# One stage for merge and output product, a search that turns bits by exclusive or, and units placed anew

## The chip, the cores and the metric

One core of a Trainium2 chip runs the whole program. The metric is the device time of one execution in microseconds (us). Three timed runs of the kernel before lie between 3658.96 and 3662.44, with a median of 3660.72. The engines are named as in the profile: PE is TensorE, DVE is VectorE, ACT is ScalarE, POOL is GpSimd and SP is SyncE, which only issues DMAs here. "Clock" is the TensorE clock that was granted, as a share of full speed.

## The reference

Two transformer blocks run one after the other on 2048 tokens of width 1024. The first block selects 256 keys for each query by an index score before it attends; the second has a sliding window. Both end in the same two products: a gated merge of two branches, and an output product.

```python
def first_block(x, ...):
    proj = rms_norm(x) @ w_in
    iscore = sum_h relu(qi_h @ ki.T) * wi_h          # 8 index heads, causal by chunks of 64
    idx = top_k(iscore, 256)                         # attention over these keys alone
    a = dsa_attention(...) * silu(z_a)
    b = multiscale_pool(u_b, ...) * silu(z_b)
    g = sigmoid(gates + merge_bias)
    y = g[0] * (a @ w_branch_a) + g[1] * (b @ w_branch_b)
    return x + y @ w_out

def second_block(x, ...):
    ...
    merged = gate_a * (y_a @ w_proj_a) + gate_b * (y_b @ w_proj_b)
    y = merged @ w_out
    return x + gate * rms(y, g_post)
```

All values are float32. The kernel gets close to float32 by splitting each operand into a high part (rounded to the fp32r type) and a low part (the rest), and by three matmuls: high by high, high by low, low by high.

## The kernel before, in words

The program is a chain of phases, each with its own buffers and its own block of instruction streams, joined by semaphores. Two kinds of phase are touched.

**phase_first** computes the z, u and gate columns of the input projection (the "units"), the index scores, and the key masks. There are 112 units: 56 for each half of the tokens. A unit is 128 columns by 512 tokens, that is 8 steps of k with three matmuls each, 24 matmuls of 128x512. A "place" is one block of 128 weight columns; it serves two units. Its weights are loaded (w_raw), rounded by ACT (w_hi, line 1043) and the low part (w_lo) is a subtraction, made by DVE (line 1115) where it falls in an index stretch and by POOL (line 1033, four instructions of 128x256) elsewhere. There are three slots for split weights, so place m can be split when place m - 3 is done. The low part is needed two places, or about four units, after its slot came free.

The 16 query tiles are handled in two halves of seven (two short tiles need no search). Each half has an index stretch and a try stretch:

- Index stretch: 88 "heads". PE multiplies queries by up to 1024 keys (line 1260) into one of two PSUM buffers, ACT applies relu (line 1066) into one of two buffers, DVE scales and adds (line 1133 for the first head, 1136 for the others). Units are laced between the heads on PE by `slices`; their PSUM is emptied by ACT (lines 1053, 1055, 1057), and a z unit has one more DVE multiplication (line 1124). `IDX_UNITS` says which units stand in the stretch, `FROM` from which head on.
- Try stretch: a search for the 256th largest score of every query, bit by bit, 32 tries. In each try ACT counts three tiles by Sign with an accumulated sum (line 1073), DVE counts four tiles by a comparison (line 1145), and then three short DVE instructions of 128x7 make the next level: `enough` (line 1161), `prefix` (1165) and `level` (1168). The next try's counts wait for it. `TRY_UNITS` says which units stand beside the tries; PE streams them without a wait on the search, but ACT empties their PSUM (four buffers) only between its counts, in the order of `beside_try`.

After the tries, `settle` (lines 1175 to 1184) corrects the level, and `make_mask` (lines 1194 to 1205) makes one mask per tile: for half 0 in front of the heads of half 1, for half 1 at the end of the phase. The order on each engine is the order in which the program emits it; nothing is planned at run time. The activations of a half (p_hT) are loaded again for half 1: SP issues these loads when it comes to units 53 and 56.

**phase_output** runs once for each block, as two blocks of streams with separate buffers. `merge_branches` takes 32 units (4 groups of 512 tokens by 8 column blocks), 24 matmuls each, with the weights as the stationary operand; DVE multiplies by the gates (line 1814) and adds (1816) into yT. `output_product` then loads w_out in eight pieces of 512 KB through two slots (line 1685), rounds them on ACT (1690), makes the low parts in turn on DVE (1696) and POOL (1702), splits y by tile (1904, 1886) and multiplies: 16 tiles of 128 tokens, 48 matmuls each (lines 1948 to 1950) with y as the stationary operand, into one of two PSUM buffers. The first pass over k goes as far as the weights are there.

Of the kernel before, what the change touches and what calls it, by code (L numbers as in the profile page):

```python
# [12 lines left out]
ALU = mybir.AluOpType  # L13
# [803 lines left out]
def phase_first(c, stack):  # L817
# [38 lines left out]
    IDX_UNITS = [(0, 21), (57, 77)]  # L856
    TRY_UNITS = [(21, 57), (77, 107)]
# [42 lines left out]
    cand = sb("cand", [P, NB], I32)  # L900
# [4 lines left out]
    enough = sb("enough", [P, NB], I32)  # L905
# [27 lines left out]
    with nc.Block() as block:  # L933
# [90 lines left out]
        def _(pool):  # L1024
# [87 lines left out]
        def _(dve):  # L1112
# [35 lines left out]
            def begin(half, step):  # L1148
# [3 lines left out]
                nc.vector.memset(prefix[:], 0)  # L1152
# [3 lines left out]
            def attempt(half, j, step):  # L1156
                for b in range(NACT, NB):
                    last = count(half, b, ALU.is_lt)
                step(last)
                dve.wait_ge(counted, half * TRIES + j + 1)  # L1160
                step(nc.vector.tensor_tensor(enough[:], counts[:], wanted[:], ALU.is_le))
                if j == 0:
                    step(nc.vector.tensor_scalar(turned_bits[:], enough[:], -1.0, None, ALU.add))
                else:
                    step(nc.vector.scalar_tensor_tensor(out=prefix[:], in0=enough[:], scalar=TRY_OF[j - 1], in1=prefix[:],
                                                        op0=ALU.logical_shift_left, op1=ALU.bitwise_or))
                if j < TRIES - 1:
# [3 lines left out]
                    dve.wait_ge(cand_ready, half * TRIES + j + 2)  # L1171

            def settle(half, step):
# [3 lines left out]
                step(nc.vector.tensor_tensor(cand[:], prefix[:], upd[:], ALU.add))  # L1177
                step(nc.vector.tensor_tensor(level[:].bitcast(I32), cand[:], turned_bits[:], ALU.bitwise_xor))
# [533 lines left out]
def phase_output(c, stack, second):  # L1712
# [3 lines left out]
    sb, _, _ = c.alloc(stack, "o2" if second else "o1")  # L1716
    yT = sb("yT", [P, KD, SEQ], F32)
    with ExitStack() as inner:
        merge_branches(c, inner, second, yT)
    with ExitStack() as inner:  # L1720
        output_product(c, inner, second, yT)


# [753 lines left out]
```

## Time and profile before

| | us |
|---|---|
| median of three timed runs | 3660.72 |
| the profiled execution | 3663.65 |
| its span, first to last instruction | 3661.9 |
| PE busy | 3227.8 (88%) |
| DVE busy | 1772.6 (48%) |
| ACT busy | 1566.7 (43%) |
| POOL busy | 1162.2 (32%) |
| mean granted clock | 0.927 |

Busy time is a mean over stages with different limits. A share of 88% on PE says that PE is the engine to look at first; it does not say that it is the limit in each stage. The phases that the change touches are phase_first, from about 336 to 1127 us, and the two output phases, from about 1697 to 2130 and from about 3215 to the end.

### The profile page before, as it was taken

To read this page: it belongs to the slowest core of one execution; us is meant where nothing else is said; L and a number is where in the kernel's file an instruction comes from. 1 tells how busy PE (TensorE), PEld (TensorE's weight loads), DVE (VectorE), ACT (ScalarE), POOL (GpSimd) and SP (SyncE) were. 2 spreads that over 40 slices of the span, in tenths; PEclk is the share of its full clock that TensorE was granted. 3 is DMA by queue.
4 is the path that set the end of the run, shared out by engine and by line. 5 is a ranking of instruction groups with operands and counts; after the bars stand their busy time and mean duration, and the time that the engine had idled before them with its cause. 6 is when DMAs were issued, how large, how long until landed. Compare 5 with 4: busy or idle time off the path is not lost. (4 is left out here: it accounts for less than half of the span.)

```text
span 3661.9 us, 43478 instructions
## 1 busy us (share of the span) xinstructions
PE 3227.8 (88%) x15878; PEld 2639.9 (72%) x15878; DVE 1772.6 (48%) x3727; ACT 1566.7 (43%) x2453; POOL 1162.2 (32%) x780
## 2 busy tenths in 40 slices
PE   3996999789983999967897959997999999978799
PEld 3995888677773677755675848886888888856587
DVE  3775679988995666532331126661312132123222
ACT  2444568756973677721101023333444354420111
POOL 2441002200222899922212223332222222232132
PEclk9997999999996999967998969998999999989899
DMA  4566333433324111055543244546444634354422
GB/s 113 173 194 210 119 98 92 146 119 90 92 81 135 61 61 37 27 175 192 144 104 115 92 138 141 159 135 222 124 128 153 208 122 134 110 146 124 117 84 92
DMA packets 419821, 458.19 MB, mean 125 GB/s; under 512 B 30896, under 2 KB 301744, under 8 KB 417968
## 3 DMA queue, kind: packets, MB, share of 16 engines
q1 hardware_dynamic: 419632, 455.72, 40.4%
q8 instruction: 113, 1.85, 0.2%
q14 instruction: 76, 0.62, 0.1%
HBM read 289.70 MB, written 165.94 MB: 124 GB/s over the span
## 5 line engine op out<-in xcount | busy, mean ns | idle before, releaser
L1411 POOL TENSOR_SCALAR a_prob<-a_prob,a_inv 128x128 f32<-128x128 f32 (+15 forms) x128 | 384.2, 3020 | 96.3 <-DVE a_inv L1452 96.2
L1243 PE MATMUL p_pr<-p_hT,p_w_hi 128*128 128x512 f32 x896 | 359.2, 401 | 27.3 <-POOL p_w_lo L1033 26.9
L2324 PE MATMUL p_pr<-p_hT,p_w_hi 128*128 128x512 f32 x896 | 352.2, 393 | 17.6 <-DMA p_hT<-s_hT 17.6
L1244 PE MATMUL p_pr<-p_hT,p_w_hi 128*128 128x512 f32 x896 | 356.3, 398 | 0.0
L1245 PE MATMUL p_pr<-p_hT,p_w_lo 128*128 128x512 f32 x896 | 355.5, 397 | 0.0
L2325 PE MATMUL p_pr<-p_hT,p_w_hi 128*128 128x512 f32 x896 | 350.3, 391 | 0.0
L2326 PE MATMUL p_pr<-p_hT,p_w_lo 128*128 128x512 f32 x896 | 349.7, 390 | 0.0
L758 PE MATMUL t_pj_ps<-t_w_hi,t_hT_slot 128*128 128x356 f32 (+2 forms) x768 | 274.1, 357 | 41.0 <-POOL t_w_lo L474 26.6
L1033 POOL TENSOR_TENSOR p_w_lo<-p_w_raw,p_w_hi 128x256 fp32r<-128x256 f32 x132 | 93.1, 736 | 651.9 <-ACT p_w_hi L1043 651.9
L1073 ACT ACTIVATE p_relu<-p_isc,p_level 128x2048 int8<-128x2048 f32 (+5 forms) x192 | 276.7, 1442 | 43.2 <-DVE p_level L1168 41.8
L1833 PE MATMUL m_b_ps<-m_in_hi,m_w_hi 128*128 128x512 f32 x512 | 214.1, 418 | 77.2 <-POOL m_in_lo L1791 46.2
L760 PE MATMUL t_pj_ps<-t_w_hi,t_hT_slot 128*128 128x356 f32 (+2 forms) x768 | 266.8, 347 | 0.0
L759 PE MATMUL t_pj_ps<-t_w_lo,t_hT_slot 128*128 128x356 f32 (+2 forms) x768 | 266.6, 347 | 0.0
L1432 DVE CUSTOM_DVE_ANT_0 a_prob<-a_s_ps,a_mask 128x512 f32<-128x512 f32 (+3 forms) x320 | 188.5, 607 | 152.3 <-PE a_s_ps L1511 148.8
L1948 PE MATMUL f_o_ps<-f_w_hi,f_y_hi 128*128 128x512 f32 x512 | 207.1, 404 | 42.3 <-POOL f_w_lo L1702 22.0
L2171 POOL TENSOR_TENSOR p_w_lo<-p_w_raw,p_w_hi 128x1024 fp32r<-128x1024 f32 x56 | 136.3, 2434 | 330.4 <-ACT p_w_hi L2193 330.4
L1511 PE MATMUL a_s_ps<-a_kT,a_qT 128*128 128x512 f32 (+3 forms) x640 | 197.8, 414 | 35.9 <-DMA a_kT<-s_kT 30.8
L1145 DVE TENSOR_SCALAR_CACHE_REDUCE p_ranks<-p_isc,p_level 128x1792 uint8<-128x1792 f32 (+4 forms) x130 | 223.0, 1752 | 2.6 <-DVE p_level L1153 0.4
L1243 PEld LDWEIGHTS p_pr<-p_hT,p_w_hi 128*128 128x128 f32 x896 | 172.6, 193 | 69.1 <-POOL p_w_lo L1033 31.3
L1490 ACT ACTIVATE a_pt<-a_t_ps 128x512 f32<-128x512 f32 x272 | 153.7, 593 | 134.2 <-PE a_t_ps L1523 133.6
L2324 PEld LDWEIGHTS p_pr<-p_hT,p_w_hi 128*128 128x128 f32 x896 | 168.8, 188 | 58.2 <-POOL p_w_lo L2171 14.8
L1834 PE MATMUL m_b_ps<-m_in_lo,m_w_hi 128*128 128x512 f32 x512 | 209.1, 408 | 0.0
(270 smaller groups left out, 7142.2 us busy)
## 6 DMA issues: line engine op xcount, KB each, us to landing
p_w_raw<-in_w_in SPq DMA_DIRECT2D x112, 512.0 KB, 4.3
s_hT<-t_hT_slot SPq DMA_DIRECT2D x32, 1024.0 KB, 5.9
p_hT<-s_hT SPq DMA_DIRECT2D x64, 512.0 KB, 9.8
s_gT<-p_o_sb SPq DMA_DIRECT2D x128, 256.0 KB, 4.9
m_gates<-s_gT SPq DMA_DIRECT2D x64, 512.0 KB, 4.9
s_qT<-t_qT_slot SPq DMA_DIRECT2D x32, 512.0 KB, 2.7
s_zuT<-p_o_sb SPq DMA_DIRECT2D x64, 256.0 KB, 5.0
pl_wada<-in_w_ada SPq DMA_DIRECT2D x6, 2048.0 KB, 14.1
```

Source lines behind the costliest of these rows:

```text
L758: nc.tensor.matmul(o, hi, wh, start=(k == 0), stop=False)
L759: nc.tensor.matmul(o, hi, wl, start=False, stop=False)
L760: last = nc.tensor.matmul(o, lo, wh, start=False, stop=(k == KD - 1))
L1073: last = nc.scalar.activation(unread[:, o:o + w], isc[:, o:o + w], ACT.Sign, scale=-1.0, bias=level[:, b:b + 1], accum_out=counts[:, b:b + 1])
L1145: return nc.vector.tensor_scalar(unread[:].bitcast(mybir.dt.uint8)[:, at:at + w], isc[:, o:o + w], level[:, b:b + 1], None, op, ALU.add, a ...
L1243: nc.tensor.matmul(pr[n % NPR][:], wh, hi, start=(k == 0), stop=False)
L1244: nc.tensor.matmul(pr[n % NPR][:], wh, lo, start=False, stop=False)
L1245: last = nc.tensor.matmul(pr[n % NPR][:], wl, hi, start=False, stop=(k == KD - 1))
L1411: nc.gpsimd.tensor_scalar(prob[:, slot, 0:n], prob[:, slot, 0:n], inv[:, slot:slot + 1], None, ALU.mult).then_inc(normed, 1)
L2324: nc.tensor.matmul(pr[n % NPR][:], wh, hi, start=(k == 0), stop=False)
L2325: nc.tensor.matmul(pr[n % NPR][:], wh, lo, start=False, stop=False)
L2326: last = nc.tensor.matmul(pr[n % NPR][:], wl, hi, start=False, stop=(k == KD - 1))
```

## The change

1. **Units.** `IDX_UNITS` goes from (0, 21), (57, 77) to (0, 15), (52, 72), and `TRY_UNITS` from (21, 57), (77, 107) to (15, 52), (72, 106). So the index stretches hold 15 and 20 units (21 and 20 before), the try stretches 37 and 34 (36 and 30), and 6 are left behind them (5).
2. **Search.** `prefix` is no longer kept; the level itself is carried. A try computes `flipped` (the level with the next bit set or turned) before it waits for ACT's counts, then `short` and the new level by a shift and an exclusive or. `settle` gets the prefix back with one more instruction.
3. **POOL's low parts.** Where POOL makes low parts beside the tries, it now also waits for the level of the next try (`cand_ready`).
4. **Output phases.** Merge and product become one block of streams. w_out is loaded in column-block pieces over the merge's low weights, each when the merge's unit that used that block last is done (the last eight units); high parts go over the merge's high weights, low parts in place. DVE makes the low parts 0, 2, 4, 6 and 7, POOL 1, 3 and 5. y is split into ring slots that the last group does not use. The product has four PSUM buffers, and reads its weights as four pieces of 128 columns.

```diff
-    IDX_UNITS = [(0, 21), (57, 77)]
-    TRY_UNITS = [(21, 57), (77, 107)]
+    IDX_UNITS = [(0, 15), (52, 72)]
+    TRY_UNITS = [(15, 52), (72, 106)]
+    def split_try(m):
+
+        n = last_unit(m - SLOTS_W) + 1
+        return [half * TRIES + j for half in range(2) for j in range(TRIES) if n in beside_try(half, j)]
...
                     pool.wait_ge(w_hi_done, m + 1)
+                    for e in split_try(m):
+                        if e % TRIES < TRIES - 1:
+                            pool.wait_ge(cand_ready, e + 2)
...
+                bits = level[:].bitcast(I32)
+                if 0 < j < TRIES - 1:
+                    step(nc.vector.tensor_scalar(flipped[:], bits, 1 << TRY_OF[j], None, ALU.bitwise_xor))
                 dve.wait_ge(counted, half * TRIES + j + 1)
-                step(nc.vector.tensor_tensor(enough[:], counts[:], wanted[:], ALU.is_le))
+                step(nc.vector.tensor_tensor(short[:], counts[:], wanted[:], ALU.is_gt))
                 if j == 0:
-                    step(nc.vector.tensor_scalar(turned_bits[:], enough[:], -1.0, None, ALU.add))
+
+                    step(nc.vector.tensor_scalar(turned_bits[:], short[:], -1.0, None, ALU.mult))
+                    ins = nc.vector.tensor_scalar(bits, turned_bits[:], 1 << TRY_OF[0], None, ALU.bitwise_xor)
                 else:
-                    step(nc.vector.scalar_tensor_tensor(out=prefix[:], in0=enough[:], scalar=TRY_OF[j - 1], in1=prefix[:],
-                                                        op0=ALU.logical_shift_left, op1=ALU.bitwise_or))
+
+                    ins = nc.vector.scalar_tensor_tensor(out=bits, in0=short[:], scalar=TRY_OF[j - 1],
+                                                         in1=flipped[:] if j < TRIES - 1 else bits,
+                                                         op0=ALU.logical_shift_left, op1=ALU.bitwise_xor)
                 if j < TRIES - 1:
-                    nc.vector.scalar_tensor_tensor(out=level[:].bitcast(I32), in0=prefix[:], scalar=1 << TRY_OF[j],
-                                                   in1=turned_bits[:], op0=ALU.bitwise_or, op1=ALU.bitwise_xor
-                                                   ).then_inc(cand_ready, 1)
+                    ins.then_inc(cand_ready, 1)
                     dve.wait_ge(cand_ready, half * TRIES + j + 2)
...
+            def load_wo(k):
+
+                sp.wait_ge(weighed, LAST + k + 1)
+                sp.dma_start(wo_part(wo_raw, k), wo[0, k * P:(k + 1) * P, :].rearrange("p (j n) -> p j n", n=P)
+                             ).then_inc(wo_loaded[k], 16)
...
+                if u >= LAST:
+                    load_wo(u - LAST)
...
+            low(0)
+            low(1)
+            for k in range(1, KD - 1, 2):
+                pool.wait_ge(wo_hi_done, k + 1)
+                nc.gpsimd.tensor_tensor(wo_part(w_lo, k), wo_part(wo_raw, k), f32(wo_part(w_hi, k)), ALU.subtract
+                                        ).then_inc(wo_lo_done[k], 1)
...
+            high(0)
+            high(1)
+            for k in range(KD):
+                act.wait_ge(wo_loaded[k], 16)
+                nc.scalar.activation(wo_part(w_hi, k), wo_part(wo_raw, k), ACT.Copy).then_inc(wo_hi_done, 1)
...
+                if u >= LAST + 2 and (u - LAST) % 2 == 0:
+                    low_weights(u - LAST - 2)
+            low_weights(KD - 2)
+            low_weights(KD - 1)
...
+                pe.wait_ge(y_lo_done, t + 1)
+                if t < NO:
+                    pe.wait_ge(multiplied, UNITS_ALL - NO + t + 1)
                 else:
+                    pe.wait_ge(out_done, t - NO + 1)
+                for j in range(2):
+                    o, part = b_ps[t % NO][:, j], slice(j * KB, (j + 1) * KB)
                     for k in range(KD):
                         if t == 0 and j == 0:
-                            ready(pe, k)
+                            pe.wait_ge(wo_lo_done[k], 1)
+                        wh, wl = wo_part(w_hi, k)[:, part], wo_part(w_lo, k)[:, part]
+                        nc.tensor.matmul(o, y_hi[:, s, k], wh, start=(k == 0), stop=False)
+                        nc.tensor.matmul(o, y_hi[:, s, k], wl, start=False, stop=False)
+                        last = nc.tensor.matmul(o, y_lo[:, s, k], wh, start=False, stop=(k == KD - 1))
```

## Rows read from the trace of the kernel before

**Rows 1.** Stretches: start:end length, PE PEld DVE ACT POOL busy, clock, DMA share, GB/s.
```profile
370.00:509.40 139.40, 139.01 (x622) 114.74 (x621) 90.16 (x113) 77.85 (x103) 0.00 (x0) 1.00 0.36 108
509.40:722.20 212.80, 200.68 (x864) 163.95 (x862) 206.08 (x358) 183.93 (x246) 48.03 (x69) 0.97 0.37 106
739.90:894.40 154.50, 142.64 (x613) 115.20 (x612) 131.78 (x166) 89.45 (x127) 0.00 (x0) 0.97 0.32 100
894.40:1078.80 184.40, 172.34 (x737) 140.62 (x736) 179.97 (x351) 166.92 (x237) 39.61 (x57) 0.96 0.31 86
```
**Rows 2.** Waits of the first try stretch: engine tile line <- what ended it: us, times, longest.
```profile
PE p_pr L1243 <- POOL p_w_lo L1033: 12.1, 5, 7.4
DVE p_enough L1161 <- ACT p_relu L1073: 0.7, 1, 0.7
```
**Rows 3.** Timeline of PE in the first try stretch: start, duration.
```profile
600.21 0.39 PE L1243 MATMUL p_pr<-p_hT,p_w_hi 128*128 128x512 f32 x1
...
600.89 0.39 PE L1243 MATMUL p_pr<-p_hT,p_w_hi 128*128 128x512 f32 x1
```
**Rows 4.** Timelines of DVE and POOL, half 0: a try with a collision, and one without.
```profile
515.77 2.08 DVE L1145 TENSOR_SCALAR_CACHE_REDUCE p_ranks<-p_isc,p_level 128x1792 uint8<-128x1792 f32 x1
...
521.37 2.83 POOL L1033 TENSOR_TENSOR p_w_lo<-p_w_raw,p_w_hi 128x256 fp32r<-128x256 f32 x4 [184.88 <-ACT p_w_hi L1043]
521.43 0.70 DVE L1165 SCALAR_TENSOR_TENSOR p_prefix<-p_enough,p_prefix 128x7 int32<-128x7 int32 x1
522.16 0.66 DVE L1168 SCALAR_TENSOR_TENSOR p_level<-p_prefix,p_turned_bits 128x7 int32<-128x7 int32 x1
522.86 2.08 DVE L1145 TENSOR_SCALAR_CACHE_REDUCE p_ranks<-p_isc,p_level 128x1792 uint8<-128x1792 f32 x1
...
528.91 2.08 DVE L1145 TENSOR_SCALAR_CACHE_REDUCE p_ranks<-p_isc,p_level 128x1792 uint8<-128x1792 f32 x1
```
**Rows 5.** Try stretches, DVE busy in line 1165 (first row), then line 1168.
```profile
509.40:722.20 212.80, 13.76 (x31) 0.97 0.37 106
...
509.40:722.20 212.80, 12.56 (x31) 0.97 0.37 106
894.40:1078.80 184.40, 12.86 (x31) 0.96 0.31 86
```
**Rows 6.** Timelines of DVE and ACT: end of try stretch 0; one try of half 1.
```profile
721.57 0.69 DVE L1124 TENSOR_TENSOR p_o_sb<-p_pr,p_o_sb 128x512 f32<-128x512 f32 x1 [1.48 <-ACT p_o_sb L1055]
...
928.70 1.90 ACT L1073 ACTIVATE p_relu<-p_isc,p_level 128x1920 int8<-128x1920 f32 x1 [0.69 <-DVE p_level L1168]
932.87 1.05 ACT L1043 ACTIVATE p_w_hi<-p_w_raw 128x1024 fp32r<-128x1024 f32 x1
933.82 0.67 ACT L1057 ACTIVATE p_o_sb<-p_pr,keep_mbias 128x512 f32<-128x512 f32 x1
```
**Rows 7.** Chain of waits at the second product's start (DMA), and DVE's timeline there.
```profile
3451.53 4.93 DMA f_raw<-in_w_out
...
3474.07 3.58 DMA f_raw<-in_w_out
...
3474.38 1.22 DVE L1696 TENSOR_TENSOR f_w_lo<-f_raw,f_w_hi 128x1024 fp32r<-128x1024 f32 x1 [5.55 <-ACT f_w_hi L1690]
```
**Rows 8.** Timeline around both products' starts: last merge matmul, first tile's end.
```profile
1922.84 0.39 PE L1835 MATMUL m_b_ps<-m_in_hi,m_w_lo 128*128 128x512 f32 x1
1964.54 1.06 ACT L1904 ACTIVATE f_y_hi<-o_yT 128x1024 fp32r<-128x1024 f32 x1 [10.73 <-PE f_o_ps L1950]
3448.48 0.39 PE L1835 MATMUL m_b_ps<-m_in_hi,m_w_lo 128*128 128x512 f32 x1
3490.36 1.03 ACT L1915 ACTIVATE f_x_out<-f_o_ps 128x1024 f32<-128x1024 f32 x1 [10.68 <-PE f_o_ps L1950]
```
**Rows 9.** Timeline of PE in the attention phase; line 1536 reads two pieces of 128 columns.
```profile
1504.00 1.95 PE L1536 MATMUL a_o_ps<-a_pt,a_v 128*64 128x256 f32 x16
1505.87 0.73 PE L1511 MATMUL a_s_ps<-a_kT,a_qT 128*128 128x512 f32 x2
```

More of the change, by code:

```diff
@@ L904, in phase_first @@
     counts = sb("counts", [P, NB], F32)
-    enough = sb("enough", [P, NB], I32)
+    short = sb("short", [P, NB], I32)
+    flipped = sb("flipped", [P, NB], I32)
     wanted = sb("wanted", [P, NB], F32)
@@ L1176, in settle @@
                 step(nc.vector.memset(wanted[:], float(TOPK)))
-                step(nc.vector.tensor_tensor(cand[:], prefix[:], upd[:], ALU.add))
-                step(nc.vector.tensor_tensor(level[:].bitcast(I32), cand[:], turned_bits[:], ALU.bitwise_xor))
+                step(nc.vector.tensor_tensor(prefix[:], level[:].bitcast(I32), turned_bits[:], ALU.bitwise_xor))
+                step(nc.vector.tensor_tensor(flipped[:], prefix[:], upd[:], ALU.add))
+                step(nc.vector.tensor_tensor(level[:].bitcast(I32), flipped[:], turned_bits[:], ALU.bitwise_xor))
                 for b in range(NACT):
@@ L1792, in _, with high @@
                                         ).then_inc(lo_done, 1)
+            low(0)
[4 more added lines that the diff above has]
+                                        ).then_inc(wo_lo_done[k], 1)
+            for t in range(T):
+                if t >= 1 and t + 1 < T:
+                    low(t + 1)
+                if second:
+                    s = t % 2
+                    pool.wait_ge(squared, t + 1)
+                    nc.gpsimd.tensor_tensor(stat[:, s, 1:2], stat[:, s, 0:1], c.eps[:, 0:1], ALU.add).then_inc(meaned, 1)
+                    pool.wait_ge(meaned, t + 1)
+                    nc.gpsimd.tensor_tensor(stat[:, s, 2:3], stat[:, s, 1:2], c.minus_half[:, 0:1], ALU.pow).then_inc(powered, 1)
         @block.scalar
         def _(act):
+            def high(t):
+                if t >= 2:
+                    act.wait_ge(produced, t - 1)
+                else:
+                    act.wait_ge(weighed, LAST)
+                    act.wait_ge(summed, GROUPS)
+                nc.scalar.activation(y_hi[:, t % 2], tile(t), ACT.Copy).then_inc(y_hi_done, 1)
             for x in range(GROUPS * KD):
@@ L1805, in _, with low_weights @@
                 nc.scalar.activation(in_hi[:, x % RING], src[:, x % 2], ACT.Copy).then_inc(hi_done, 1)
+            high(0)
[3 more added lines that the diff above has]
+                nc.scalar.activation(wo_part(w_hi, k), wo_part(wo_raw, k), ACT.Copy).then_inc(wo_hi_done, 1)
+            act.wait_ge(summed, UNITS_ALL)
+            for t in range(T):
+                if t >= 1 and t + 1 < T:
+                    high(t + 1)
+                if second:
+                    act.wait_ge(produced, t + 1)
+                    if t >= 2:
+                        act.wait_ge(out_done, t - 1)
+                        act.wait_ge(stored[t % 2], 16 * (t // 2))
+                    nc.scalar.activation(x_out[:, t % 2], o_ps(t), ACT.Square, scale=D ** -0.5,
+                                         accum_out=stat[:, t % 2, 0:1]).then_inc(squared, 1)
         @block.vector
         def _(dve):
+            def low_weights(k):
+                dve.wait_ge(wo_hi_done, k + 1)
+                nc.vector.tensor_tensor(wo_part(w_lo, k), wo_part(wo_raw, k), f32(wo_part(w_hi, k)), ALU.subtract
+                                        ).then_inc(wo_lo_done[k], 1)
             vector(dve, range(KD))
@@ L1936, in _ @@
-        @block.tensor
-        def _(pe):
-            for t in range(T):
-                s = t % 2
-                pe.wait_ge(lo_done, t + 1)
-                if t >= 2:
-                    pe.wait_ge(out_done, t - 1)
-                for j in range(D // BANK):
-                    cols = slice(j * BANK, (j + 1) * BANK)
+                pe.wait_ge(y_lo_done, t + 1)
+                if t < NO:
+                    pe.wait_ge(multiplied, UNITS_ALL - NO + t + 1)
+                else:
+                    pe.wait_ge(out_done, t - NO + 1)
```

175 lines of the change are left out of this document (66 added, 109 removed).

## The prediction

> **What bounds the kernel now.** The page's engine totals come first: PE is busy for 88% of the span, so work taken off another engine pays only where PE waits for it. The busy times by stretch then say where that is. From 370 to 509 us PE is busy 139.0 of 139.4 us while DVE is busy 90: this index stretch is PE's [rows 1]. In both try stretches DVE is busy 97 to 98% (206.1 of 212.8 us, 180.0 of 184.4) and PE has holes: the search sets the pace there [rows 1]. PE's longest wait in the first of them is for the weights' low part, 12.1 us in 5 times, and DVE waited for ACT's counts once, 0.7 us [rows 2]. Low parts come late only because ACT empties units in the search's order; the wait is a symptom. In the index stretch of half 1 PE (142.6) and DVE (131.8) share 154.5 us, neither full [rows 1]. At the two output phases the timeline shows PE's last merge matmul and the end of the first product tile, and a hole between them in which w_out is fetched [rows 8].
>
> **Unit of account.** Matmuls of 512 columns follow each other at (600.89 - 600.21) / 3 = 0.2267 us [rows 3], so a unit of 24 takes 5.44 us and a product tile of 48 takes 10.88 us. All sums are made on the profiled execution, 3663.65 us (span 3661.9), which lies 2.9 us above the median of the timed runs.
>
> **1. Output phases.** Before, the merge's last matmul starts at 1922.84 and is streamed by 1923.07; the first tile ends at 1964.54, so at full pace it would have begun at 1953.66: 30.6 us are lost. The second time it is 3448.71 to 3490.36 - 10.88 = 3479.48, 30.8 us [rows 8]. Now seven of the eight w_out pieces can come while the merge's last seven units run (38 us). The last piece cannot: its room is free only at the merge's end. It costs SP's issue (0.35, as I read issues of this kind), the transfer (3.58 in the old chain, 4.93 with a second load in flight; the two x tiles are issued right behind it, so I take 4.3) [rows 7], ACT's rounding (1.05) [rows 6], DVE's low part (1.22) [rows 7] and some 0.3 us of semaphores, 7.2 us. PE has seven k steps of 0.68 us to do before it needs that piece, 4.8 us. The hole is 2.4 us; piece 6, freed one unit earlier, is in time. Behind DVE's low parts 0, 2 and 4 stands its gate multiplication, but DVE needs 1.9 + 1.2 us of 5.44 per unit there, and PE has four PSUM buffers. POOL's three low parts and the y splits lie beside the merge's last units too. Gain 28.2 + 28.4 = **-56.6**. Ends: no hole at all (-61), or each piece late by another 5 us (-47).
>
> The product now reads its moving operand as four pieces of 128 columns. No matmul of this length does that before. The nearest row is line 1536, with two pieces: 16 of 256 columns in 1505.87 - 1504.00 = 1.87 us, 0.117 each, where half of 0.2267 is 0.113 [rows 9]. I take 0. The upper end is 0.004 x 3 for each of 1536 matmuls, +18 us; nothing in the row would make them faster, so the lower end is 0. The rest of the steady product (18 stores, squares, norms) is the same work at the same pace, with more buffers.
>
> **2. First index stretch.** Six units fewer are 32.6 us off PE [rows 1, 3]. Left from 370 us on: 139.0 - 32.6 = 106.4 on PE. DVE loses three low parts (1.22 each) and a z multiplication (0.69) [rows 6, 7]: 90.2 - 4.4 = 85.8. PE still sets the end, but with 81% on DVE and two buffers between each pair of engines it will not be full. The second index stretch shows PE at 92% with DVE at 85% and long mask blocks in it [rows 1]; without masks I give back 3 us. **-29.6**, ends -32.6 and -20.6 (PE at 90%, as a bound near that stretch).
>
> **3. First try stretch.** A try takes 528.91 - 522.86 = 6.05 us when POOL is quiet, and 7.09 us when a burst of POOL's low parts (2.83 us) begins beside `prefix` and `level`: these take 0.70 and 0.66 instead of 0.17 [rows 4]. Over 31 tries the excess is 13.76 + 12.56 - 62 x 0.168 = 15.9 us [rows 5]. After the change POOL starts with the next counts, which last about 5.3 us, longer than its burst; 18 bursts fit. The last z unit leaves this stretch as well: 1.5 us wait and 0.7 [rows 6]. So the search would take 32 x 6.05 = 193.6 in place of 212. PE now has 37 units, 201.3 us, and becomes nearly the limit: 35 of them (190.4 us, begun some 3 us before the search) must be emptied before the last counts can start at 31 x 6.05 = 187.6. That is a tie; I add 0.8. **-17.4**. PE ends about 4 us behind the search, under `settle` and the first mask (together 17 us).
>
> **4. Second try stretch.** Only `level` collides there: 12.86 - 31 x 0.168 = 7.7 us [rows 5]. 34 units must stand beside 177 us of search; 32 of them before the last counts, 174.1 - 3 + 0.6 = 171.7 against 31 x 5.52 = 171.1. ACT's own load in a try with a split is 4.17 (counts) + 0.95 + 0.6 = 5.7 us [rows 6], 0.2 over the try, and ACT's counts are 0.8 us shorter than DVE's, so this doesn't reach the level. I give back 0.7. **-7.0**.
>
> **5. The exclusive or.** DVE's counts end last, so `flipped` isn't hidden: three short instructions in line before, three after (the old three took 3 x 0.2 us). 0, and -0.2 us per try, -12 in all, if ACT were always last. `settle` gains one instruction and loses two collisions: -1 over both halves.
>
> **6. Second index stretch and tail.** 20 units as before, one more z (0.7 us). New in it is the load of half 1's activations (issued at units 53 and 56, needed three units, some 20 us, later); before it lay mostly beside tries. I take 0; ends -5 and +12. Behind the tries PE has two units not yet run and six more, 43.5 us from about 4 us before the search's end; `settle` and the masks need 47 us there, and ACT's sides wait for each mask anyway: 0.
>
> Sum: -56.6 - 29.6 - 17.4 - 7.0 - 1.0 = -111.6, or 3552.0 us for the profiled execution, and about 3549 for the median. I say **3550**.
>
> **A rule that speaks against step 3.** The counts of line 1145 take 2.08 us at 515.77, with POOL quiet, and 2.08 us at 522.86, with POOL's burst running until 524.20 [rows 4]. They don't feel POOL; `prefix` does. The Trainium skill (SBUF — State Buffer, Terms) has VectorE and GpSimd share a port pair under an exclusive lock, where the loser "fully blocks". Taken for every instruction, it would put each burst on top of a count. The Trainium skill (GPSIMD Engine Reference, the row on SBUF interfaces) narrows this to VectorE instructions in a two-port mode or with two SBUF inputs; the counts have one tensor input, `prefix` has two. By that narrower rule the trace agrees.
>
> **Rivals.** (a) *The pieces pull the pace down in the product (slower).* Place: 1536 matmuls. If pieces of 128 columns streamed at half pace the price is 0.2267 x 1536 = 348 us, 3898 us; it decides from 111 / 1536 = 0.07 us per matmul. Against it: 0.004 us in line 1536 [rows 9]. (b) *Counts are held up by POOL's bursts.* 18 + 17 bursts x 2.83 = +99: 3649 us. Against it: the equal 2.08 us [rows 4]. (c) *The freed index time is given back.* With 12 us more in the first index stretch, 12 in the second by the activation load: 3574. For it: PE's 92% in the second [rows 1]. (d) *POOL's bursts still meet the short instructions*, because ACT's rounding comes late when it waits for PE: steps 3 and 4 lose 24 us, 3574. Against it: a burst begun late by 2 us still ends inside the counts. (e) *w_out comes late.* 5 us more per hole and a few us of pace: 3563. (f) *Everything overlaps better*: no give-back in steps 2 to 4 and a better second index stretch, 3540.
>
> **Chances.** Forecast 0.50, (a) 0.02, (b) 0.02, (c) 0.15, (d) 0.07, (e) 0.10, (f) 0.12, that the change does nothing visible 0.02. The range of 8 in 10 is 3537 to 3576. A measurement of this kernel tells 0.2%, 7 us, from no change. Faster by over that: all but (a) and the last, 0.96 less what is unnamed, 0.95; within 0.02; slower 0.03.
>
> **What would show it.** Right: the first product tile ends about 13 us after the merge's last matmul, twice, with the granted clock at 1.0 between; the first count of half 0 starts near 480 us; tries at 6.05 and 5.52 us with no 0.7 us instruction of 128x7; PE without a hole over 2 us in either try stretch. Wrong: a matmul pace over 0.23 us in the product (a), counts over 2.1 us beside POOL (b), PE under 95% from 370 us to the first count (c), bursts over `short` (d), a hole over 5 us at the product's start (e).

## The result: 3571.05 us, where 3550 was forecast

| kernel | median of its runs | ratio to before (95% interval) |
|---|---|---|
| before | 3659.84 us (4 runs, 3656.10 to 3662.44) | |
| after | 3571.05 us (4 runs, 3569.73 to 3572.50) | 0.9758 (0.9742 to 0.9773) |

The change takes 88.8 us off the median, 2.4%. The profiled execution of after has a span of 3569.3 us, 92.6 less than the 3661.9 of before. The time is inside the range of 3537 to 3576, but 21 us above the forecast: of 111.6 us worked out, some 19 are missing. Before any experiment the trace says in which steps. The parts in the table run from the first count of a search to its `settle`, and so on; the tail ends with the last mask.

| part | before | after | change | forecast |
|---|---|---|---|---|
| start to the first count of half 0 | 509.7 | 478.7 | -31.0 | -29.6 |
| first try stretch | 212.5 | 201.9 | -10.6 | -17.4 |
| second index stretch, with `settle` and the first masks | 172.2 | 179.9 | +7.7 | 0 |
| second try stretch | 184.4 | 179.6 | -4.8 | -7.0 |
| tail: second `settle` to the last mask | 45.9 | 49.6 | +3.7 | -1 or 0 |
| all that follows | 2537.2 | 2479.6 | -57.6 | -56.6 |

The two big terms hold to 1.4 us. The last of them is less sharp than it looks: behind the last mask, kernels with the same code there take from 2473.6 to 2482.5 us in their profiled executions. What is missing lies between the first count of half 0 and the last mask.

### The profile after

Busy times by stretch, after; columns as in [rows 1], and the stretches answer to those there:
```profile
370.00:478.70 108.70, 108.12 (x483) 87.93 (x482) 86.08 (x108) 70.81 (x95) 0.00 (x0) 1.00 0.36 107
478.70:680.60 201.90, 199.33 (x880) 164.72 (x878) 190.58 (x352) 182.82 (x247) 49.00 (x70) 1.00 0.34 94
697.80:860.50 162.70, 145.41 (x617) 115.90 (x616) 133.44 (x167) 90.47 (x127) 0.00 (x0) 0.96 0.46 143
860.50:1040.10 179.60, 179.60 (x794) 148.79 (x793) 172.38 (x351) 168.59 (x242) 45.43 (x65) 1.00 0.36 101
```
The first number behind the length is PE. It stays full in the first index stretch (108.1 of 108.7 us) with 31 us less to do, as step 2 had it. In the try stretches it has gone from holes to 99 and 100%. In the second index stretch (third row; its start is the settle and mask that [rows 1] leaves out too) PE's own work grew by 2.8 us and the stretch by 8.2, and the DMA share rose from 0.32 to 0.46.

The 0.7 us instructions. DVE's busy time in line 1178 (`level`), first try stretch, then second; they answer to [rows 5]:
```profile
478.70:680.60 201.90, 5.68 (x31) 1.00 0.34 94
860.50:1040.10 179.60, 5.16 (x31) 1.00 0.36 101
```
31 x 0.167 is 5.18: one instruction in the first stretch still takes 0.68 us, that of the last try, which GpSimd's wait leaves out. Every other burst of the tries now lies beside the counts. The counts don't feel it, as [rows 4] said: with a burst from 521.87 to 524.69, DVE's timeline has
```profile
521.56 0.17 DVE L1178 SCALAR_TENSOR_TENSOR p_level<-p_short,p_flipped 128x7 int32<-128x7 int32 x1
521.76 2.08 DVE L1153 TENSOR_SCALAR_CACHE_REDUCE p_ranks<-p_isc,p_level 128x1792 uint8<-128x1792 f32 x1
...
527.22 0.17 DVE L1169 TENSOR_SCALAR p_flipped<-p_level 128x7 int32<-128x7 int32 x1
529.00 0.17 DVE L1171 TENSOR_TENSOR p_short<-p_counts,p_wanted 128x7 int32<-128x7 f32 x1 [1.60 <-ACT p_relu L1081]
```
The last row is where step 3's missing time is: DVE is through with its counts at 527.18 and stands 1.60 us for ACT's. The waits of the first try stretch, those of DVE, ACT and PE that matter; they answer to [rows 2]:
```profile
DVE p_short L1171 <- ACT p_relu L1081: 7.1, 4, 1.9
...
ACT p_o_sb L1065 <- DMA s_gT<-p_o_sb: 6.6, 3, 2.2
ACT p_o_sb L1061 <- DMA s_zuT<-p_o_sb: 2.1, 1, 2.1
...
PE p_pr L1258 <- POOL p_w_lo L1041: 4.6, 1, 4.6
```
PE's wait for the low part fell from 12.1 us to 4.6, the last of them begun in this stretch and ended 2 us behind it. But ACT now waits for stores, 8.7 us in four pieces, and DVE waits for ACT in the same four tries. Before had this wait too, shorter; it is one row of the same view as [rows 2], of the first try stretch:
```profile
ACT p_o_sb L1057 <- DMA s_gT<-p_o_sb: 3.4, 3, 1.4
```
One of these three stood just ahead of the single 0.7 us that DVE waited for ACT in [rows 2]. The timelines of POOL, SP's queue and ACT ahead of the first one show how:
```profile
515.81 2.83 POOL L1041 TENSOR_TENSOR p_w_lo<-p_w_raw,p_w_hi 128x256 fp32r<-128x256 f32 x4 [9.29 <-DVE p_level L1178]
...
518.67 0.38 SPq L946 DMA_DIRECT2D p_w_raw<-in_w_in  x1
519.10 1.06 SPq L970 DMA_DIRECT2D s_zuT<-p_o_sb  x2
...
523.84 0.60 ACT L1061 ACTIVATE p_o_sb<-p_pr 128x512 f32<-128x512 f32 x1 [2.13 <-DMA s_zuT<-p_o_sb]
524.33 1.99 ACT L1081 ACTIVATE p_relu<-p_isc,p_level 128x2048 int8<-128x2048 f32 x1
```
POOL's burst begins with the counts and ends at 518.64. SP's queue is in order, and a unit's turn there is "load the next weight tile, then store the unit before last"; the load waits for the low part, so it goes out at 518.67 and the stores only behind it. ACT needs the slot of one of them, waits 2.13 us, and starts its counts at 524.33 where DVE began at 521.76. That is still a reading; the experiments test it.

The second index stretch. Timelines of ACT, of SP's queue and of PE there:
```profile
733.53 0.68 ACT L1065 ACTIVATE p_o_sb<-p_pr,keep_mbias 128x512 f32<-128x512 f32 x1
...
745.39 0.38 SPq L946 DMA_DIRECT2D p_w_raw<-in_w_in  x1
745.82 0.58 SPq L970 DMA_DIRECT2D s_gT<-p_o_sb  x1
746.44 6.99 SPq L954 DMA_DIRECT2D p_hT<-s_hT  x8
```
```profile
755.48 0.50 PE L1258 MATMUL p_pr<-p_hT,p_w_hi 128*128 128x512 f32 x1 [0.53 <-DMA p_hT<-s_hT]
...
758.70 0.79 PE L1258 MATMUL p_pr<-p_hT,p_w_hi 128*128 128x512 f32 x1 [2.26 <-DMA p_hT<-s_hT]
759.29 0.63 PE L1259 MATMUL p_pr<-p_hT,p_w_hi 128*128 128x512 f32 x1
```
ACT empties the last unit of half 0 at 733.53, but the second group of half 1's activations is issued at 746.44, again behind a weight load, and PE reaches the first unit that reads them at 752. It waits piece by piece, 3.5 us in four waits, and the matmuls behind are of 0.63 us instead of 0.39: the granted clock is 0.79 from 754 to 762. Step 6 had this load 20 us ahead of its use. Before, the second group was issued at 725.99 us, in the second index stretch as well, but beside `settle` and the first mask, where PE had little to stream (8.8 of the 17.7 us from 722.2 on); only the first group lay beside the tries. After has both groups in this stretch, the first at 702.27.

The output phases. Timeline of PE and ACT around the second product's start, which answers to [rows 8], and a stretch of its steady part:
```profile
3382.68 0.39 PE L1955 MATMUL o_b_ps<-o_in_hi,o_w_lo 128*128 128x512 f32 x1
...
3397.76 1.03 ACT L1900 ACTIVATE o_gates<-o_b_ps 128x1024 f32<-128x1024 f32 x1 [9.43 <-PE o_b_ps L1972]
```
```profile
3400.00:3500.00 100.00, 100.00 (x443) 82.86 (x442) 32.73 (x20) 18.57 (x27) 30.39 (x28) 1.00 0.27 95
```
The merge's last matmul is streamed by 3382.91 and the first tile's end is 14.9 us later, where it was 41.7: a hole of 4.0 us instead of 30.8. In the first output phase it is 1887.63 to 1900.66, 13.0 us and a hole of 2.2. The forecast had "about 13 us". Some 2 us of the 4.0 are no wait: the granted clock was 0.51, the lower of its two levels, from 3390 to 3393, behind PE's two short waits for low parts, and matmuls followed each other at 0.43 us there. After's second profiled execution has 13.2 us at this place, with the clock at 1.00. In the steady part 443 matmuls take 100 us, 0.2257 each: reading four pieces of 128 columns costs nothing.

The tail has one row that no step foresaw. POOL's last low part, beside DVE's scan and masks:
```profile
1040.06 2.83 POOL L1041 TENSOR_TENSOR p_w_lo<-p_w_raw,p_w_hi 128x256 fp32r<-128x256 f32 x4 [7.87 <-ACT p_w_hi L1051]
1050.58 8.81 POOL L1041 TENSOR_TENSOR p_w_lo<-p_w_raw,p_w_hi 128x256 fp32r<-128x256 f32 x4 [7.68 <-ACT p_w_hi L1051]
```

### The profile page after: what moved, and what is told of

It is laid out like the page before. It is cut to its first block and busy times, and to the rows that moved or that the text cites. A ratio compares the mean times of both kernels' runs of the same rounds, so it can differ in the third digit from the quotient of the medians.

```text
span 3569.3 us, 43493 instructions
## 1 busy us (share of the span) xinstructions
PE 3204.4 (90%) x15878; PEld 2629.3 (74%) x15878; DVE 1759.3 (49%) x3726; ACT 1562.5 (44%) x2453; POOL 1171.6 (33%) x790
## 5 line engine op out<-in xcount | busy, mean ns | idle before, releaser
L1041 POOL TENSOR_TENSOR p_w_lo<-p_w_raw,p_w_hi 128x256 fp32r<-128x256 f32 x144 | 108.0, 783 | 616.1 <-DVE p_level L1178 401.9
L1953 PE MATMUL o_b_ps<-o_in_hi,o_w_hi 128*128 128x512 f32 x512 | 214.9, 420 | 74.3 <-POOL o_in_lo L1848 45.4
L1954 PE MATMUL o_b_ps<-o_in_lo,o_w_hi 128*128 128x512 f32 x512 | 209.7, 410 | 0.0
L1955 PE MATMUL o_b_ps<-o_in_hi,o_w_lo 128*128 128x512 f32 x512 | 208.8, 408 | 0.0
```

The costliest lines, as they stand in the source:

```text
L1953: nc.tensor.matmul(o, w_hi[:, k, cols], in_hi[:, x % RING], start=first, stop=False)
```

## The experiments

Each was timed in five rounds against the kernel before on the same chip, whose median lay between 3655.0 and 3657.2 us. The ratios are therefore what is compared: after has 0.9758, one thousandth is 3.7 us, and each interval reaches 1.3 to 1.4 thousandths to either side. Lengths of stretches come from one profiled execution each.

### After, once more

> After itself, unchanged, as the partner of load_first_alone on the same chip and as a second look at its parts: 3567 to 3573 us, second index stretch 177 to 182 us.

Measured: 3566.0 us, ratio 0.9757 (0.9743 to 0.9770): by the ratio the same as before, though the median is 1 us under what was expected, on a chip whose kernel before was quicker too. First count 478.9, then 201.6, 180.8, 179.6 and a tail of 49.2 us. Stretches repeat within 1 us here, and what follows the last mask within 5.4; two kernels below with the same code in the second index stretch (180.5 and 177.9 us) differ by more, so 3 us in that stretch is no verdict by itself.

### The output stage by itself

Edit: before, with only the functions of the output phases taken from after.

> Before, with only the merged output stage of the change. Theory A (the two output phases gave their 56.6 us in full, and what fell short of the forecast lies in the search phase): 3659.8 - 56.6 = 3603, within 3 us. Rival B (the output stage gave less, and the trace of after only shows it because other stages shifted): above 3610, at least 7 us of the missing 23.

Measured: 3603.2 us, ratio 0.9846 (0.9832 to 0.9859), 56.3 us less than before. The search keeps its times (try stretches 212.4 and 184.3, last mask at 1125.2). Theory A holds: the output stage gave what step 1 says, to the 5 us of the interval, and what is missing is in the search phase. The second index stretch, with before's own code, is 174.7 us here for 172.2.

### The units where they were

```diff
-    IDX_UNITS = [(0, 15), (52, 72)]
-    TRY_UNITS = [(15, 52), (72, 106)]
+    IDX_UNITS = [(0, 21), (57, 77)]
+    TRY_UNITS = [(21, 57), (77, 107)]
```

> After, with the units placed as before, (0, 21), (57, 77) and (21, 57), (77, 107). Theory A (the second index stretch, the ends of the try stretches and the tail are late because of where the units now lie): the first index stretch gets its 31 us back, but the first try stretch loses 7, the second index stretch 7.4, the second try stretch 2.2 and the tail some of its 3.7, so +11 to +15 and 3582 to 3586. Rival B (these losses come from the new search or from GpSimd's wait and stay whatever the placement): +29 to +31, so 3600 to 3602.

Measured: 3586.1 us, ratio 0.9800 (0.9787 to 0.9814), 15 us above after. First index stretch 508.8, first try stretch 204.0, second index stretch 173.4, second try stretch 177.1, tail 46.5. So 6.5 of the 7.7 us of the second index stretch and 3 of the tail's 3.7 come from the placement, A. So does step 4's loss: with 30 units the second try stretch is 7.3 us shorter than before, and the four units more cost 2.5. One part of A missed: the first try stretch does not lose 7 us, it is 204.0. With only 36 units the new wait is still there (its waits in the first try stretch):
```profile
DVE p_short L1171 <- ACT p_relu L1081: 5.8, 3, 2.2
...
ACT p_o_sb L1065 <- DMA s_gT<-p_o_sb: 7.0, 3, 2.7
```
So this wait does not come from the one unit more. Whether it comes from the order in which things are issued is tested below.

### GpSimd without its wait

```diff
                     pool.wait_ge(w_hi_done, m + 1)
-                    for e in split_try(m):
-                        if e % TRIES < TRIES - 1:
-                            pool.wait_ge(cand_ready, e + 2)
```

> After, with GpSimd's wait for a try's start taken out (its low part again starts as soon as ScalarE has split). Theory A (the wait keeps the bursts off the short instructions, and its price is that the low part is late): 16 bursts cost up to 1.0 us each again, +15.9 at most, ScalarE's waits for a free o_sb slot (8.7 and 2.6 us) go, net +5 to +10, so 3576 to 3581. Rival B (the bursts have shifted and would miss the short instructions anyway): the waits go and nothing comes back, -5 to -9, so 3562 to 3566. Rival C (TensorE with 37 units sets the first try stretch whatever DVE does): no change within 2 us in that stretch, +2 to +5 in the second, so 3573 to 3576.

Measured: 3581.4 us, ratio 0.9792 (0.9779 to 0.9805), 12 us above after. The try stretches are 210.7 and 186.8 us, 16.0 more than with the wait. `short`, the first instruction behind ACT's counts, in the first try stretch:
```profile
478.00:688.00 210.00, 13.26 (x32) 0.98 0.33 90
```
13.26 us for 32 against 5.34 in after: the bursts meet `short` and the instruction behind it again (13.08 us for 31), and B is out. ACT's waits for stores fall from 8.7 to 3.6 us, so the wait does have the price that A gives it, though not all of it. C is out too: PE's 37 units did not hold the first stretch at 201.9.

### The store ahead of the load

In SP's turn for a unit:
```diff
+                if n >= 2:
+                    store(n - 2)
                 for m in split_at(n):
                     if m + 2 < 2 * CHUNKS:
                         load_w(m + 2)
-                if n >= 2:
-                    store(n - 2)
```

> After, with SyncE issuing a unit's store ahead of the load of the next weight tile, where it came behind it. Theory A (in the try stretches the load waits for GpSimd's low part and holds the store back, the ring of four o_sb slots runs out, ScalarE comes late to its counts): ScalarE's waits for the stores go from 8.7 us to under 2 in the first try stretch and from 2.6 to 0 in the second, and the time falls by 6 to 10 us, to 3561 to 3565. Rival B (TensorE is saturated there: 37 units of 5.44 us are 201.3 us): the waits go and the time stays within 1.5 us of 3571.

Measured: 3559.6 us, ratio 0.9726 (0.9712 to 0.9739), 11 us below after, a little more than expected. The first try stretch is 197.1 us (201.9), the second 178.9 (179.6). ACT and DVE in the first try stretch; a wait of ACT for a store is no longer among its rows:
```profile
ACT p_o_sb L1065 <- PE p_pr L1260: 5.2, 4, 2.1
...
DVE p_short L1171 <- ACT p_relu L1081: 2.2, 2, 1.7
```
Nothing was changed but the order of two entries of one queue, so this settles the cause of 4.8 of the 6.8 us that step 3 missed. What is left of ACT's waits is for PE: 37 units are 201.3 us, the near tie that step 3 spoke of. By stretches the profile places 6.7 of the 11 us: 4.8, 0.7 and 1.2 in the tail. The rest is not placed. The second stretch, with PE full in both kernels, gains only 0.7. Rival B was wrong in the first stretch and nearly right in the second.

### The activation load left out

```diff
-                if n == N_HALF - LEAD:
-                    load_h(1, 0)
-                if n == N_HALF:
-                    load_h(1, 1)
```

> After, without the load of the second half's activations into hT: the second half's units multiply the first half's data (their results are left wrong; the work is the same). Theory A (the second index stretch is 7.7 us longer than before because this load now lies in it: TensorE and ScalarE wait for hT, 5.2 us in one piece at 755 to 761): the stretch falls from 179.9 to 172 to 174 us, the whole to 3563 to 3566. Rival B (the stretch is longer because the try stretch before it hands on unfinished units of a TensorE that was 100% busy): it stays above 178, the whole above 3569.

Both groups are left out, and PE's wait for them. Measured: 3557.8 us, ratio 0.9726 (0.9713 to 0.9739). The second index stretch is 173.7 us, the try stretches 202.3 and 179.5 as in after. The load is worth 6.2 of the 7.7 us in this pair of executions; the other kernels with these units and the load lie between 176.9 and 181.5. Theory A holds for the stretch; the whole fell by 12 us, 6 more than the stretch explains. The profile places 1.5 of these before the first count and 5.5 behind the last mask, where after's second execution is 5.4 us shorter too with no change at all; so nothing but the stretch can be put down to the load.

### The old decision

```diff
-                    step(nc.vector.tensor_scalar(flipped[:], bits, 1 << TRY_OF[j], None, ALU.bitwise_xor))
...
-                step(nc.vector.tensor_tensor(short[:], counts[:], wanted[:], ALU.is_gt))
+                step(nc.vector.tensor_tensor(enough[:], counts[:], wanted[:], ALU.is_le))
...
+                    step(nc.vector.scalar_tensor_tensor(out=prefix[:], in0=enough[:], scalar=TRY_OF[j - 1], in1=prefix[:],
+                                                        op0=ALU.logical_shift_left, op1=ALU.bitwise_or))
```

> After, with the try's decision as before (enough, prefix, level: three short instructions behind ScalarE's count) in place of the exclusive or (flipped ahead of it, short and level behind). Theory A (step 5 of the prediction: the chain only changes its order): 0 to +3 us, the try stretches within 1.5 us each of 201.9 and 179.6, their period near 6.06 us, as GpSimd's wait keeps the bursts off. Rival B (one short instruction fewer behind the count shortens each try by 0.2 us or more): +7 us or more over both halves. Rival C (the exclusive or, not GpSimd's wait, removed the collisions): +15 or more.

Measured: 3564.1 us, ratio 0.9747 (0.9734 to 0.9761); its interval holds after's ratio. Try stretches 202.6 and 179.4 us, against 201.9 and 179.6. Theory A, at zero for the tries: there the exclusive or neither gains nor costs, and GpSimd's wait alone took the collisions away (`level` takes 0.165 to 0.169 us in the first stretch). Outside the tries it does cost: `settle` has one instruction more, 2.02 and 2.12 us from its start to its first count in after, 1.33 and 1.42 here.

### The activation load ahead of the weight load

Made twice: on after, and on the kernel with the store first.
```diff
             def unit(n):
+                if n == N_HALF:
+                    load_h(1, 1)
                 ...
                 if n == N_HALF - LEAD:
                     load_h(1, 0)
-                if n == N_HALF:
-                    load_h(1, 1)
```

> The kernel of store_before_load (3559.6 us, second index stretch 180.5 us), with SyncE issuing the load of the second half's second group into hT ahead of that unit's store and weight load, where the weight load, which waits for the split of a buffer, came first (issued at 738.7, the activations at 739.1, though TensorE had finished the last unit that reads the old ones 12 us earlier). Theory A (the load comes late because it is queued, and what the missing load was worth, 6.2 us, is its lateness): issued 6 to 7 us earlier, TensorE's waits for hT go from 2.7 us to under 0.5, the stretch falls by 3 to 5 us to 175.5 to 177.5, the whole to 3554 to 3557. Rival B (the 6.2 us are the load's traffic and queue time wherever it lies in the stretch): the stretch stays within 1 us of 180.5.

> After, with only the load of the second group of half 1's activations issued ahead of that unit's weight load and store; no other edit. Two profiled executions with the same code in the second index stretch were 180.5 and 177.9 us, so that stretch's 3.6 us in load_first may be part scatter. Theory A (the place in the queue costs 3 to 5 us of the 6.2 of this load): TensorE's waits for hT under 0.5 us (3.5 in after), 3 to 6 us less than after timed beside it, so 3565 to 3568. Rival B (scatter): the waits go, but the time stays within 1.5 us of after's.

Measured: on the kernel with the store first 3554.8 us, ratio 0.9721 (0.9708 to 0.9734), stretch 176.9 us for 180.5. On after 3565.9 us, ratio 0.9749 (0.9736 to 0.9763), stretch 180.3 us for 180.8 in after's second execution. The first looked like theory A by its stretch and its median; by the ratio it is 1.8 us, inside the intervals. The second, beside after itself, is rival B: no difference. Yet the edit did what it says. In the second kernel the load is issued 8.3 us earlier and PE no longer waits for hT. SP's queue in it, and the one new row in ACT's waits:
```profile
738.15 7.59 SPq L954 DMA_DIRECT2D p_hT<-s_hT  x8
745.78 1.89 SPq L946 DMA_DIRECT2D p_w_raw<-in_w_in  x1
747.72 5.50 SPq L970 DMA_DIRECT2D s_gT<-p_o_sb  x2
```
```profile
ACT p_o_sb L1063 <- DMA s_gT<-p_o_sb: 6.2, 1, 6.2
```
The eight pieces hold SP's queue for 7.6 us. Behind a weight load they are late themselves; ahead of it the stores are late, and ACT waits 6.2 us for a slot of the ring (4.6 us in the kernel with the store first). The wait changed its owner. So "late because it is queued" does not explain the price: on after, the load costs as much where it is early (180.3 for 180.8). Whether it is the queue's seven microseconds or the traffic is not told apart: the two stores behind the pieces take 5.50 us to issue, where two took 1.06 at 519.10.

### The tail's two waits

Based on the kernel with the store first: ACT empties a unit one mask later, and DVE makes the last weight tile's low part.
```diff
             for b in range(NB):
                 sides(1, b)
-                if b < N_UNITS - TRY_UNITS[1][1]:
-                    unit(TRY_UNITS[1][1] + b)
+                if b and TRY_UNITS[1][1] + b - 1 < N_UNITS:
+                    unit(TRY_UNITS[1][1] + b - 1)
...
             for b in range(NB):
                 make_mask(1, b, finish)
+                if TRY_UNITS[1][1] + b < N_UNITS:
+                    unit(TRY_UNITS[1][1] + b)
```

> After with the store ahead of the load (3559.6 us), and in the tail: ScalarE evacuates a unit one mask later, so that it does not wait for TensorE ahead of a mask's side, and VectorE makes the last weight tile's low part (1.22 us) behind the first mask in place of GpSimd (8.8 us beside the scan). Theory A (these two waits and the slowed mask instructions are the tail's 2.5 us over before): tail 48.4 to 45 or 46, the whole 3556 to 3558. Rival B (the tail is VectorE's own chain of masks, 44.3 us busy of 49): within 1 us of 3559.6.

Measured: 3559.4 us, ratio 0.9735 (0.9722 to 0.9749), no faster than its base; the tail is 47.6 us (48.4). Rival B: it is DVE's chain of masks. DVE's `settle` and first mask in after, and the first mask here:
```profile
1040.24 0.57 DVE L1191 TENSOR_TENSOR p_prefix<-p_level,p_turned_bits 128x7 int32<-128x7 int32 x1
1040.85 0.67 DVE L1192 CUSTOM_DVE_ANT_0 p_flipped<-p_prefix,p_upd 128x14 uint16<-128x14 uint16 x1
1041.55 0.67 DVE L1193 TENSOR_TENSOR p_level<-p_flipped,p_turned_bits 128x7 int32<-128x7 int32 x1
...
1050.34 4.16 DVE L1211 TENSOR_TENSOR_SCAN p_ranks<-keep_ones,p_keep 128x1920 f16<-128x1920 f32 x1
...
1055.07 2.65 DVE L1215 SCALAR_TENSOR_TENSOR p_keep<-p_ranks,p_room,p_side 128x1920 bf16<-128x1920 f16 x1
1057.75 1.06 DVE L1220 TENSOR_SCALAR p_mask<-p_keep 128x1920 bf16<-128x1920 bf16 x1
```
```profile
1041.41 4.16 DVE L1213 TENSOR_TENSOR_SCAN p_ranks<-keep_ones,p_keep 128x1920 f16<-128x1920 f32 x1
...
1045.80 2.22 DVE L1217 SCALAR_TENSOR_TENSOR p_keep<-p_ranks,p_room,p_side 128x1920 bf16<-128x1920 f16 x1
1048.05 0.66 DVE L1222 TENSOR_SCALAR p_mask<-p_keep 128x1920 bf16<-128x1920 bf16 x1
1048.63 1.22 DVE L1125 TENSOR_TENSOR p_w_lo<-p_w_raw,p_w_hi 128x1024 fp32r<-128x1024 f32 x1
```
Beside POOL's burst the scan keeps its 4.16 us, and it is POOL that pays (8.8 us); the instructions behind it are slowed by 0.4 us each. Most of what DVE gets back it spends on the low part. DVE's timelines account for all of the tail's 3.7 us over before. `settle` takes 2.12 us to its first count for 1.38: it has one instruction more, and POOL's burst of 1040.06 lies beside all three (0.74). POOL's last burst slows the first two masks (1.44). Ahead of the fourth mask DVE waits 1.59 us for ACT, whose program empties a unit first and waited 9.41 us for PE to finish it (1.48). The store order took 1.2 of the last part, this edit the rest of it and 0.5 of the second. Left are 0.7 for `settle` and 0.9 at the first mask, where the low part now stands.

### Units placed again, with all of it

Based on the kernel of the tail: `IDX_UNITS = [(0, 14), (50, 71)]`, `TRY_UNITS = [(14, 50), (71, 105)]`; first without, then with the earlier activation load.

> The kernel of tail_apart with the units at (0, 14), (50, 71) and (14, 50), (71, 105): one unit fewer in the first index stretch and in the first try stretch, one more in the second index stretch, seven in the tail. Theory A (TensorE sets the first index stretch, 5.2 us a unit as the change showed; the first try stretch is TensorE's with 37 units and VectorE's with 36; the second index stretch has 13% of TensorE idle and takes one more for 1 to 4 us): -5, -1 to -3, +1 to +4, so 3551 to 3556. Rival B (the second index stretch pays the whole unit and more, 5 to 9 us, and the tail its own): 3558 to 3563, no better than tail_apart.

> The kernel of combined (3555.6 us, second index stretch 180.4 us) with the same earlier load. Theory A: the stretch 176 to 178 us, the whole 3550 to 3553. Rival B: within 1 us of 3555.6.

Measured: 3555.6 us, ratio 0.9722 (0.9708 to 0.9735), and 3549.8 us, ratio 0.9705 (0.9692 to 0.9719). The first count comes at 473.6 instead of 477.2 and the first try stretch falls from 197.2 to 195.6; the second index stretch goes from 177.9 to 180.4 with its extra unit, and to 177.8 with the earlier load, both within that stretch's scatter. With 36 units DVE has no wait for ACT left in the first try stretch. The tail falls from 47.6 to 46.2 us, because with the units placed so POOL's last burst begins at 1028.83, when `settle`'s three instructions (DVE, in `combined`) are through:
```profile
1028.31 0.17 DVE L1193 TENSOR_TENSOR p_prefix<-p_level,p_turned_bits 128x7 int32<-128x7 int32 x1
1028.52 0.17 DVE L1194 CUSTOM_DVE_ANT_0 p_flipped<-p_prefix,p_upd 128x14 uint16<-128x14 uint16 x1
1028.71 0.17 DVE L1195 TENSOR_TENSOR p_level<-p_flipped,p_turned_bits 128x7 int32<-128x7 int32 x1
```
In `combined` it is a query tile's load that stands behind the activations:
```profile
PE p_sc_ps L1279 <- DMA p_qiT<-s_qiT: 6.5, 1, 6.5
```
With the earlier load this is 1.7 us, and ACT's wait for a store 1.4: in this placement, and with the stores first, the queue's seven microseconds fall where less is waiting. The two intervals overlap, from 0.9708 to 0.9719, so the 6 us between the two are not shown. The last kernel is the fastest of all, 107 us (3.0%) below the kernel before beside it, and by the ratios 19 us below after (0.9705 against 0.9757 and 0.9758, intervals apart).

## Why the prediction was right, and where it was short

**Step 1, output phases: right.** -56.6 forecast, -57.6 in the trace, 56.3 when made alone. The holes were 2.2 and 4.0 us for 2.4 each, which is 55.2; that the trace's sum comes within 1 us is in part luck, as all that follows the last mask scatters by more. Rival (a), the pace of the pieces, is out at 0.2257 us per matmul. Rival (e)'s sign, a hole over 5 us, did not come.

**Step 2, first index stretch: right.** -31.0 for -29.6. PE stays at 99.5%, so the 3 us of give-back were 1.4 too many.

**Step 3, first try stretch: mechanism right, size off.** -17.4 forecast, -10.6 measured. The collisions went as said, but for the last try's, and most tries take 6.06 to 6.07 us. The term that failed is "POOL starts with the next counts, which last about 5.3 us, longer than its burst": it asked only what the burst would meet. It did not ask who waits for the burst's end. SP does, in the weight load, and the stores stand behind it; the ring of four runs out, ACT and then DVE are late. Exchanging two entries of that queue took the stretch from 201.9 to 197.1 us. The rest is the tie, put at 0.8: DVE still waits 2.2 us. With one unit fewer as well the stretch is 195.6 and no wait for ACT is left; 195.1 was forecast. The trace of before had a sign of it that the prediction did not use, ACT's 3.4 us for stores. The prediction calls PE's wait for the low part a symptom and does not look at SP, which waits for the same low part. (The parts of the term add up to 17.3, 15.9 + 1.5 + 0.7 - 0.8, not 17.4; it changes nothing.)

**Step 4, second try stretch: -4.8 for -7.0.** With 30 units beside it the new search takes 177.1 us, 7.3 less than before, so the collisions were priced rightly and the units were not. One wait of ACT for a store (2.6 us) is step 3's cause again. With it gone the stretch is 178.9; there PE is at 100%, and this tie costs more than the 0.7 given back.

**Step 5, the exclusive or: right at zero in the tries, wrong in `settle`.** 0.5 us over both stretches when undone. The -1.0 that the sum has for this step came out as +1.4: from its start to its first count `settle` took 2.02 and 2.12 us for 1.38 and 1.38. Its instruction more was there; its "two collisions" fewer were not, as POOL's burst still lies beside it in both halves.

**Step 6, second index stretch and tail: wrong.** 0 forecast, +7.7 and +3.7 measured. The step that failed is "issued at units 53 and 56, needed three units, some 20 us, later". It looked at the event that permits the load and not at its way through SP's queue: it is issued 13 us after ACT began to empty unit 55, it takes 7 us to issue, and whatever stands behind it is late in turn. Without this load the stretch is 6.2 us shorter. Being late is not what it costs, though: issued 8.3 us earlier it cost the same. Nor was its place before as said: the second group was in this stretch before, too, only in a part where PE had little to do. The upper end of +12 did cover it. The tail's 3.7 us are `settle`'s 0.7, POOL's last burst beside the masks, 1.4, and DVE's wait for ACT, 1.5; "ACT's sides wait for each mask anyway" had it that ACT is never late there.

**The rivals.** (c) and (d) were the nearest in time, 3574 for 3571.05, and neither is what happened. Of (c) one half is wrong: nothing came back in the first index stretch, 7.7 us in the second by the very load that it names. So (c)'s nearness is luck. (b) and (d) are out: counts at 2.08 us beside a burst, `short` at 0.17. (f)'s 3540 was reached by none of the kernels; with one queue's order changed and the units moved once more it is 3550.

**The signs.** As announced: the first count at 478.7, tries at 6.07 and 5.53 us (medians), the steady product's pace, the first product tile 13.0 us after the first merge. Not as announced: 14.9 us and a clock of 0.88 after the second merge, one `level` of 0.68 us, and a hole of PE of 4.6 us from 678.0 on.

**The range.** Steps 3 to 6 all missed to the same side, by some 20 us together. The range held them because its upper end lies behind the 3574 of two rivals that did not come true; only the second stretch's loss was foreseen, in (c) and in step 6's +12.

## What to carry to other kernels

When an instruction is made to wait, follow its result and not only its start: list the queues in which something waits for it, and what stands behind that in order; here exchanging two entries of one queue was worth some 11 us. A short wait in the trace of before, such as ACT's 3.4 us for stores, can show which queue this is. And a transfer of many pieces holds the queue that issues it, here for seven microseconds: moving it forward may merely pass the wait on.

## What the runs showed of the hardware that was not expected

In a collision of DVE and GpSimd it is not always DVE that is slowed. Beside GpSimd's subtraction, short instructions of 128x7 with two tensor inputs take 0.70 us for 0.17, and GpSimd stays at 2.83 us [rows 4]. Beside DVE's scan of 1920 elements, which began 0.24 us ahead of the burst, the scan keeps its 4.16 us and GpSimd takes 8.81 us. What decides is not shown: the two cases differ in DVE's instruction and also in which engine had begun. The counts, with one tensor input, and GpSimd beside them keep their 2.08 and 2.83 us; but one tensor input is not enough to be spared, as the mask's bf16 instruction has one and takes 1.06 us for 0.66 beside the same burst.
